# Spreading ten half projections and the squares over the eight groups of a state-space stage

## The reference, cut to what matters

```python
h = rmsnorm(x, norm1_g[l]); proj = h @ w_in[l]
q, k, v, z, xbc, dt_raw, gate_logits = jnp.split(proj, SPLIT_POINTS, axis=-1)
...
# mamba2_bidir: 8 groups of 4 heads, both directions
y = (y_fwd + y_bwd + d_skip[:, None] * xs).reshape(b, s, SSM_INNER)
m = rmsnorm(y * jax.nn.silu(z), norm_g)          # over all 2048 channels
m_out = m @ w_ssm_br[l]
g_att, g_ssm = jnp.split(jax.nn.sigmoid(gate_logits + gate_b[l]), 2, axis=-1)
x = x + (g_att * a_out + g_ssm * m_out) @ w_out[l]
x = x + peer_ffn(rmsnorm(x, norm2_g[l]), peer_wq[l], peer_keys[l], peer_u[l], peer_v[l])
```

## Time and profile before

| | us |
|---|---|
| median of 3 runs | 2439.73 (2439.36 to 2442.9) |
| the profiled execution | 2441.23 |
| its span in the trace | 2439.4 |
| PE busy | 2091.8 (86%) |
| DVE busy | 1327.5 (54%) |
| ACT busy | 757.3 (31%) |

### The profile page before, as it was taken

One profiled execution on the slowest core, in us unless ns is written; L12 is line 12 of the kernel. 1 busy time (PEld: TensorE's weight loads), 2 busy tenths in 40 slices (PEclk: granted clock), 3 DMA queues, 4 the chain that ended last, 5 costly groups with the idle time before them and its releaser, 6 DMA issues.

```text
span 2439.4 us, 23166 instructions
## 1 busy us (share of the span) xinstructions
PE 2091.8 (86%) x8312; PEld 1338.0 (55%) x8312; DVE 1327.5 (54%) x3225; ACT 757.3 (31%) x2023; POOL 513.7 (21%) x550
## 2 busy tenths in 40 slices
PE   5999999899878787777789999999998888777776
PEld 5688888766334332222266888888663344322222
DVE  1276355417657666765413772653366667666744
ACT  2034246203332333233220432561133332333232
POOL 0000000003333333333200000000043333333331
PEclk9999999899999999999999999999999999999999
DMA  4333444438999999999913234434499999999996
GB/s 155 130 121 122 165 181 164 155 146 352 422 422 421 422 421 421 422 421 416 381 69 138 104 138 165 178 143 168 169 372 421 421 421 421 421 421 421 422 421 269
DMA packets 90403, 705.32 MB, mean 289 GB/s; under 512 B 10000, under 2 KB 10128, under 8 KB 15792
## 3 DMA queue, kind: packets, MB, share of 16 engines
q0 software_dynamic: 78400, 553.81, 55.0%
q1 hardware_dynamic: 11168, 146.36, 15.7%
q10 hardware_dynamic: 720, 3.67, 0.4%
HBM read 702.62 MB, written 1.18 MB: 289 GB/s over the span
## 4 chain that ended last, share of the span: by engine, by line
PE 55%; DMA 30%; DVE 7%; ACT 4%; issue 3%; POOL 2%; SPq 0%; DVEq 0%; POOLq 0%; ACTq 0%
DMA ring<-in_peer_uv,ex_i 29%; PE bank L408 22%; PE bank L682 11%; PE bank L393 7%; DVE ring L1349 4%; PE bank L623 3%; PE bank L590 2%; PE bank L435 2%; POOL ring L1431 2%; PE bank L567 2%; ACT diag L919 1%; PE bank L577 1%; ACT wgt L912 1%; PE bank L482 1%; PE bank L427 1%
## 5 line engine op out<-in xcount | busy, mean ns | idle before, releaser
L682 PE MATMUL bank<-ring,diag 128*128 128x512 f32 x2048 | 950.0, 608 | 264.0 <-ACT diag L919 263.7
L1349 DVE SCALAR_TENSOR_TENSOR ring<-ring,h 128x1024 f32<-128x1024 f32 x512 | 607.0, 1223 | 481.3 <-DMA ring<-in_peer_uv,ex_i 480.1
L682 PEld LDWEIGHTS bank<-ring,diag 128*128 128x128 f32 x2048 | 373.2, 191 | 812.1 <-ACT diag L919 432.3
L1431 POOL DMA_INDIRECT ring<-in_peer_uv,ex_i x512 | 494.9, 967 | 1047.2 <-PE bank L682 677.3
L408 PE MATMUL bank<-hT,w_ring 128*128 128x256 f32 x2560 | 563.8, 380 | 2.0 <-ACT hT L713 2.0
L408 PEld LDWEIGHTS bank<-hT,w_ring 128*128 128x128 f32 x2560 | 482.4, 190 | 72.4 <-issue 6.4
L906 ACT ACTIVATE gel<-act_u 128x2 f32<-128x2 f32 x256 | 52.0, 203 | 844.2 <-DVE ring L1349 840.6
L919 ACT ACTIVATE diag<-cst,wgt 128x128 f32<-128x128 f32 x512 | 177.5, 394 | 24.0 <-PE bank L682 15.8
L912 ACT ACTIVATE wgt<-gel,gate_w 128x1 f32<-128x1 f32 x512 | 122.9, 287 | 9.3
L1402 POOL DMA_DIRECT2D cs_rows_dram<-cs_rows x2 | 1.3, 662 | 580.0 <-DVE cs_rows L1122 580.0
L1077 DVE SCALAR_TENSOR_TENSOR c_tmp<-xbc,par_all,c_tmp 128x254 f32<-128x254 f32 (+1 forms) x256 | 112.3, 480 | 4.6
(11 more groups left out here) (192 smaller groups left out, 1703.8 us busy)
## 6 DMA issues: line engine op xcount, KB each, us to landing
w_ring<-in_w_stream SPq DMA_DIRECT2D x62, 2048.0 KB, 8.2
fbuf<-cs_rows_dram POOLq DMA_DIRECT2D x32, 512.0 KB, 5.9
wq<-in_w_stream SPq DMA_DIRECT2D x4, 2048.0 KB, 8.2
ring<-in_peer_uv,ex_i POOLq DMA_INDIRECT x512
out<-in_w_stream SPq DMA_DIRECT2D x2, 2048.0 KB, 12.6
keys<-in_keys_t ACTq DMA_DIRECT2D x2, 1024.0 KB, 4.7
x_tok<-in_x SPq DMA_DIRECT2D x1, 1024.0 KB, 5.3
g2row<-in_norm_rows ACTq DMA_DIRECT2D x2, 512.0 KB, 6.2
```

The lines of the kernel that those rows point to most:

```text
L682: ins = pe.matmul(bank[b0 + n][:], diag[:, PAIR * (m % 2) + s, :], ring[:, slot, DM + n * 512:DM + (n + 1) * 512], start=False, stop=True, ...
L1349: ins = dve.scalar_tensor_tensor(out=row, in0=row, scalar=1.0, in1=h2[:, b, :], op0=ALU.mult, op1=ALU.mult, accum_out=act_u[:, b, PAIR * k ...
L1431: pool.indirect_dma_start(ring[:, PAIR * q + s, :], None, peer_uv, bass.IndirectOffsetOnAxis(ap=ex_i[:, b, j:j + 1], axis=0))\
```

## The change

The ten halves are dealt out singly: one ahead of the loop, one in each of the eight groups, one behind it. In group `g` the half stands ahead of `c_times_b(g + 1)`, as the first of the two did. ACT's asides follow: one ahead of the loop, one in each group, one behind. The squares are no longer made behind the loop: ACT squares group `g - 1` at the end of its turn `g`, PE sums the squares of group `g - 2` behind the y of group `g` (into bank 7, not 4), and DVE multiplies group `g - 2` with the gain at the end of its turn `g`. The squares go into the tiles of `xbc` that the group no longer needs, so `y_sq2` goes away, and with it ACT's wait for its two slots. `m_scaled` is counted by group. No arithmetic is added or taken away.

```diff
-                beside = [C_Z + 1, C_Z + 2, C_Z + 3, C_GSSM, C_GSSM + 1]
+                def beside(n):
+                    half(C_Z + 1 + n // 2, n % 2, M_Z + 2 + n)
+
+                def sum_squares(g):
+                    wait(ysq_ready, g + 1, L)
+                    for u in range(2):
+                        ins = pe.matmul(bank[7][:, 0:SEQ], ones, xbc[:, 2 * g + u, :],
+                                        start=(g == 0 and u == 0), stop=(g == GROUPS - 1 and u == 1))
+                    ins.then_inc(ysq_used.sem, 1)
+
+                beside(0)
                 for g in range(GROUPS):
                     p = g % 2
-                    if g < len(beside):
-                        half(beside[g], 0, M_Z + 2 + 2 * g)
+                    beside(g + 1)
                     if g + 1 < GROUPS:
                         c_times_b(g + 1)
...
-                    if g < len(beside):
-                        half(beside[g], 1, M_Z + 3 + 2 * g)
-
-                for i in range(XT // 2):
-                    wait(ysq_ready, i + 1, L)
-                    for u in range(2):
-                        ins = pe.matmul(bank[4][:, 0:SEQ], ones, y_sq2[:, i % 2, u, :],
-                                        start=(i == 0 and u == 0), stop=(i == XT // 2 - 1 and u == 1))
-                    ins.then_inc(ysq_used.sem, 1)
-                wait(m_scaled, 1, L)
+                    if g >= 2:
+                        sum_squares(g - 2)
+                beside(GROUPS + 1)
+                sum_squares(GROUPS - 2)
+                sum_squares(GROUPS - 1)
+                wait(m_scaled, GROUPS, L)
...
+                def squares_of(g):
+                    wait(yz_ready, g + 1, L)
+                    act.activation(xbc[:, 2 * g:2 * g + 2, :], zT[:, 2 * g:2 * g + 2, :], ACT.Square)\
+                        .then_inc(ysq_ready.sem, 1)
+
+                aside(M_Z + 2)
                 for g in range(GROUPS):
                     if g + 1 < GROUPS:
                         cross_exps(g + 1, 4)
                         block_exps(g + 1, (0, 1))
-                    if g < 5:
-                        aside(M_Z + 2 + 2 * g)
+                    aside(M_Z + 3 + g)
                     if g + 1 < GROUPS:
                         cross_exps(g + 1, 5)
                         block_exps(g + 1, (2, 3))
                         cross_cb(g + 1)
-                    if g < 5:
-                        aside(M_Z + 3 + 2 * g)
...
+                    if g >= 1:
+                        squares_of(g - 1)
+                squares_of(GROUPS - 1)
+                aside(M_Z + 11)
...
+                def scaled(g):
+                    wait(ysq_ready, g + 1, L)
+                    for t in (2 * g, 2 * g + 1):
+                        ins = dve.tensor_scalar(zT[:, t, :], zT[:, t, :], param("sng", t, 1), None, ALU.mult)
+                    ins.then_inc(m_scaled.sem, 1)
...
+                    if g >= 2:
+                        scaled(g - 2)
                 skip_and_gate(GROUPS - 1)
...
+                scaled(GROUPS - 2)
+                scaled(GROUPS - 1)
```

More of the change, by code:

```diff
@@ L195, in encoder_kernel @@
         s_tmp, a3 = place(temps, "s_tmp", [P, 4, SEQ])
-        y_sq2, _ = place(temps, "y_sq2", [P, 2, 2, SEQ])
         r_bc, _ = place(temps + 8192, "r_bc", [P, SEQ])
@@ L305, in encoder_kernel @@
         yrms_ready = sem("yrms_ready", 1)
-        m_scaled = sem("m_scaled", 1)
+        m_scaled = sem("m_scaled", GROUPS)
         peer_loaded = sem("peer_loaded", 32)
@@ L1199, in _ @@
                         decay_times_cb(g + 1)
+                    if g >= 2:
+                        scaled(g - 2)
                 skip_and_gate(GROUPS - 1)
[L1202 to L1208, removed]
+                scaled(GROUPS - 2)
+                scaled(GROUPS - 1)
+                wait(ysq_used, GROUPS, L)
+                dve.tensor_scalar(r_bc[:], bank[7][:, 0:SEQ], 1.0 / INNER, EPS, ALU.mult, ALU.add)\
                     .then_inc(yms_ready.sem, 1)
```

## The result

The changed kernel takes 2413.15 us (median of four runs, 2410.11 to 2414.75) against 2440.19 us for the kernel before on the same chip: a ratio of 0.9886, 95% interval 0.9871 to 0.9901. The forecast was 2411.6 in a range of 2408 to 2420. In the profiled executions the span went from 2439.4 to 2411.8 us. The chips on which the runs were made differ by a few us (2437 to 2443 for the kernel before), so each run is compared with the kernel before on its own chip.

The account below looks back on a forecast made before the run. PE was taken to bound groups 0 to 4, with pauses and slow clock in 5 to 7. Two layers give 14.1 + 14.0 = 28.1 us off the 2439.73 median: 2411.6 us, own range 2409 to 2414, stated range 2408 to 2420.

Parts of the forecast that it names:

- Where PE is the bound and where not: Stage of the groups: too much PE work in groups 0 to 4, too little in 5 to 7.
- The sum of PE's work: First half to branch projection: matmuls without waits at upper clock take 105.2 us against 119.27, 14.1 less each layer.
- dealing them singly changes nothing: The ten halves: five pairs at 14.01 us make 70.05, and single halves of 6.91 or 7.12 us cost the same.
- The same number from the other side: PE's losses in the last groups and the squares' sums: 14.1 us a layer, half waiting and half slow clock.
- only the waits go: Rival, stage of the groups: small matmuls might not hold the clock up; gain 14 us, 2425; chance 0.07.
- No wait of PE: Stage in the new order: the other engines keep PE's pace of 11.5 us a group, so PE never waits.
- T + 4.5: Each group: `cbm` is copied 4.5 us after the end of the group's half; PE wants it at 11.5.
- T + 6.2: Each group: `m_ready` comes 6.2 us after the end of the group's half; PE wants it at 12.4.
- DVE's air: Each group: DVE's work of 10.6 us fits PE's 11.5, keeping pace by 0.9 us.
- the cushion: Each group: the half stands between `m_ready` and its use by PE, leaving some 6 us.
- ACT and DVE as the bound: Rival, stage of the groups: dearer table switches make the round 12.8 us, costing 4 us a layer, 2419 to 2420; chance 0.09.
- Slower, or no change: Rivals: engines in series, 72 us slower, 2512, chance 0.03; late branch projection weights give the time back, chance 0.03.

Follow-up runs that it names:

- The halves alone: The kernel before with the ten halves and their asides dealt out singly, squares, sums and scaling left behind the groups: 2419.5 us, 0.9905.
- the squares alone: The changed kernel with the halves put back in pairs beside groups 0 to 4, squares, sums and scaling still made group by group: 2440.39 us, 0.999.
- the shifted kernel: The changed kernel with 128 bytes left empty in each partition ahead of the tiles of the stage and the expert layer: 2395.41 us, 0.9817.

## Why the prediction was right, point by point

*Where PE is the bound and where not.* Right. The halves alone gave 11.2 us a layer, the squares alone 0.8 and 3.3 in the two layers, and the whole 13.5: the groups without a half were what cost.

*The sum of PE's work.* 105.2 us predicted, 105.8 measured. The term that was mis-sized is "dealing them singly changes nothing", with the 0.86 us for a sum of squares. The first matmuls behind a group's y take 0.2 us more, as a half (7.10 for 6.91) or as a sum (1.06 for 0.86). In the kernel before five halves stand behind a y, and their 0.2 us is in the 14.01 of a pair; in the changed one all eight groups have something behind y, and the three more make 0.6 us. Moving the sum moved the 0.2 us to the half and left the stretch as it was. The projection began at 443.51 us for 441.9 forecast: 0.6 of it is this term, and 1.1 is that the stretch began later, at 337.75 for 336.67, of which the cause is open.

*The same number from the other side.* The sum was right, its reading was not. I counted 7.1 us of waits and 7.0 us of slow clock as two losses of one kind. Filling the pauses brought the clock to 1.00 and only 2.4 us. The 3.3 us of slow clock in group 6 lay beside ACT's and DVE's chain of 17.66 us and cost nothing by itself. What the change removed is that this chain lay bare (17.66 less two groups' matmuls of 3.63 us each at the upper clock, 10.4 us), and what the clock itself cost is 2.6 us in y of group 7 and at most 1.1 in the sums. Nor is a pause always followed by a slow clock, as the two layers of two runs show, so that the count of 7.0 us was a reading of this one trace. The rival "only the waits go" did not occur: the clock was 1.00 through the stretch.

*No wait of PE.* Right, with the sizes: `cbm` was copied at 389.17, 4.5 us behind the half's end at 384.64, as predicted (T + 4.5), and `m_mat` was ready at 390.85, T + 6.2. DVE's air is 1.12 us where I had 0.9; one product more a group was free, and three used up the cushion that I had read as 6 us, at 12.0 and 10.4 us for an expected 11.

*ACT and DVE as the bound.* It did not happen: the exponentials begin 1.30 us after their load does, hardly more than its row of 1.28, and the square needs no load. With two more loads a group it did happen and cost 9.3 us a layer: 7.5 for 7 by the rival's arithmetic, and 1.7 of slow clock that the arithmetic had left out. By the drain that the Trainium skill puts beside a load (ScalarE: Activation LUTs, What ACT_TABLE_LOAD costs), the changed kernel would have shown a longer gap between the load and the next instruction; the trace shows none. The 1.37 us of idle behind the aside's load is no such gap: it ends with the half, and in other groups it is 1.03 or 5.05 us.

*Slower, or no change.* PE met neither the series of engines nor a late chunk: `c_times_b`, y and the projection each begin where the piece ahead of them ends.

*The total.* 28.1 us predicted, 27.0 between the medians of the first comparison, 23.5 between those of another chip (2443.09 to 2419.64). The stretches of the changed kernel are the same to 0.1 us in both its profiles. What varies is what lies outside: from the first projection to the second it has 1194.1 us in one and 1198.0 in the other. The kernel before was profiled on one chip only, so for the 23.5 this is argued and not shown. That the total came within 1.1 us of the forecast on the first chip is in part luck; that the stretches did is not.

## What to carry to other kernels

Follow the chain of waits group by group: where one engine's filler is used up early, the others' latency lies bare in the groups that are left, and the last groups show it. A filler put one step ahead of its consumer is a cushion that can be measured in microseconds by adding work to the other engines until PE waits. Slow clock behind a pause need not come, and is a loss only where PE's work ends last; beside a longer chain of other engines it costs nothing. And when an experiment's time does not follow the stretch that was edited, look at what else moved: here a tile's size had moved the address of another.

## What the hardware showed that I had not expected

The gathers depend on where the tiles begin. With `ring` where the changed kernel has it, or 4096 bytes further, they ran at 421 GB/s, with it 128 or 384 bytes further at 427 GB/s; the difference is 1.4% of a phase that transfers bound, and 0.7 to 0.9% of the kernel's time (0.9817 against the 0.9886 and 0.9903 of the changed kernel's two comparisons), nearly as much as the change gave. The two long phases of the shifted kernel were 10.8 us (1187.1 against 1198.0 from projection to projection) and 12.1 us shorter, against the changed kernel's second profile on another chip; on one chip, the run with more table loads had them 9.1 and 11.4 us shorter than the run with one more product. The transfers were called busy in both cases, 1.01 of the window. By my working `ring` begins at 384 modulo 512 bytes in the changed kernel, and at 0 or 256 in the fast ones; this rests on where the free memory begins, which no run prints. The Trainium skill (DMA: Bandwidth & Descriptors, How a descriptor splits into AXI transactions) says, of reads, that a transaction must start at a multiple of 256 bytes, so that a descriptor that begins off them needs a transaction more, and that the unused bytes ahead of its start cost beats of 32 bytes. If this holds for the written side too, the runs agree with its boundary, since 256 did as well as 0. An estimate of the loss, worked out from that page for a row of 8192 bytes at 384, is 3% by its transactions (33 for 32) and 1.6% by its beats (260 for 256), and the trace shows 1.4%. The runs show only that the shift matters, and it moves other tiles with `ring`; that it is the gathers' target, and that the transactions are the cause, is argued, not shown.

The clock need not fall behind a pause. With the squares alone, the y of group 7 follows a wait of 4.69 us in the first layer and of 3.16 in the second, and takes 5.41 us at a granted clock of 0.50 in the one and 2.87 us at 1.00 in the other. With three more products on DVE, both layers have a wait of 3.45 us there, and the y behind it takes 4.29 us at 0.64 in the first and 2.84 at 1.00 in the second. In the kernel before, both layers were slow. What decides it, these runs do not show.

The first full matmuls behind the small ones of y, which write 64 partitions each, cost 0.2 us more in these profiles (7.10 for 6.91 us in a half, 1.06 for 0.86 in a sum). The place is shown, the cause is not.
